# The opening of a two-stack kernel: shift and scale made in pairs, three unread products between pairs

## The reference

```
mod_lat = (silu_c @ ada_w[i] + ada_b[i])[:, None, :]      # 1024 x 6144, for c; the same for c_ctx
sh1, sc1, g1, sh2, sc2, g2 = jnp.split(mod_lat, 6, axis=-1)
h_lat = modulate(rmsnorm(x, norm_g[i, 0]), sh1, sc1)      # x * (1 + scale) + shift
h_ctx = modulate(rmsnorm(xc, norm_g[i, 0]), csh1, csc1)
y_ctx, y_lat = hybrid_na_sgu(h_ctx, h_lat, hyb_w_in[j], na_rpb[j], sgu_w[j], ...)
```

## Time and profile before

| | us |
|---|---|
| median of three runs | 2248.11 |
| the profiled execution | 2253.68 |
| its span | 2251.9 |
| TensorE busy | 2053.9 (91%) |
| VectorE busy | 1228.3 (55%) |
| ScalarE busy | 965.0 (43%) |
| GpSimd busy | 458.7 (20%) |
| mean granted clock of TensorE | 0.947 of full |

### The profile page before, as it was taken

The page is one execution under the profiler, slowest core; times in us unless marked ns, Lnnn a source line. Parts: engine busy times, 40 slices in busy tenths (PEclk is TensorE's granted clock), DMA queues, the critical chain, the costliest instruction groups (busy, mean ns, idle before and its releaser), DMA issues.

```text
span 2251.9 us, 34578 instructions
## 1 busy us (share of the span) xinstructions
PE 2053.9 (91%) x13471; PEld 1792.0 (80%) x13471; DVE 1228.3 (55%) x1706; ACT 965.0 (43%) x1527; POOL 458.7 (20%) x430
## 2 busy tenths in 40 slices
PE   2999979999999699999899979998799999789997
PEld 1677647777778489999799969988799989478997
DVE  1445455542454645667576857556644457875443
ACT  1534425322332432176474544366443343655343
POOL 2200013420342000021031510000082500006180
PEclk9899989999999899999999989999899999579999
DMA  9341223456432133222344444422255534023452
GB/s 300 116 164 57 101 105 131 169 170 212 151 126 89 56 115 110 76 94 94 113 161 166 169 148 169 161 102 89 99 178 177 169 131 152 18 74 133 169 170 92
DMA packets 44431, 297.00 MB, mean 132 GB/s; under 512 B 5200, under 2 KB 6480, under 8 KB 12048
## 3 DMA queue, kind: packets, MB, share of 16 engines
q1 hardware_dynamic: 36144, 245.38, 31.7%
q10 hardware_dynamic: 6336, 44.65, 5.7%
q0 software_dynamic: 1824, 5.16, 0.7%
HBM read 294.13 MB, written 1.05 MB: 131 GB/s over the span
## 4 chain that ended last, share of the span: by engine, by line
PE 82%; DVE 8%; ACT 4%; DMA 3%; POOL 2%; issue 2%; SPq 0%; ACTq 0%; POOLq 0%; DVEq 0%
PE acc L437 22%; PE acc L439 21%; PE acc L438 21%; PE wk L548 2%; DMA w_raw<-in_w_hyb_g 2%; PE acc L432 2%; PE acc L433 2%; PE acc L434 2%; PE wk L673 1%; PE wk L569 1%; PE wk L1407 1%; DVE w_lo L374 1%; DVE rstd L709 1%; ACT w_hi L365 1%; PE wk L1137 1%
## 5 line engine op out<-in xcount | busy, mean ns | idle before, releaser
L437 PE MATMUL acc<-Hhi,w_hi 128*128 128x272 f32 (+2 forms) x2320 | 749.7, 323 | 55.2 <-DVE Hlo L716 38.1
L374 DVE TENSOR_TENSOR w_lo<-w_raw,w_hi 128x1024 fp32r<-128x1024 f32 (+1 forms) x468 | 601.3, 1325 | 307.4 <-ACT w_hi L365 307.2
L439 PE MATMUL acc<-Hhi,w_lo 128*128 128x272 f32 (+2 forms) x2320 | 731.4, 315 | 0.0
L438 PE MATMUL acc<-Hlo,w_hi 128*128 128x272 f32 (+2 forms) x2320 | 730.4, 315 | 0.0
L365 ACT ACTIVATE w_hi<-w_raw 128x1024 fp32r<-128x1024 f32 (+1 forms) x468 | 451.2, 1013 | 384.9 <-PE acc L439 303.7
L437 PEld LDWEIGHTS acc<-Hhi,w_hi 128*128 128x128 f32 x2320 | 447.2, 193 | 96.8 <-issue 58.1
L438 PEld LDWEIGHTS acc<-Hlo,w_hi 128*128 128x128 f32 x2320 | 447.6, 193 | 21.4 <-issue 0.5
L439 PEld LDWEIGHTS acc<-Hhi,w_lo 128*128 128x128 f32 x2320 | 446.6, 192 | 22.3
L437 PE MATMUL acc<-Fhi,w_hi 128*128 128x272 f32 (+2 forms) x864 | 270.0, 312 | 6.9 <-POOL Flo L877 4.3
L439 PE MATMUL acc<-Fhi,w_lo 128*128 128x272 f32 (+2 forms) x864 | 268.1, 310 | 0.0
L438 PE MATMUL acc<-Flo,w_hi 128*128 128x272 f32 (+2 forms) x864 | 267.2, 309 | 0.0
(11 more groups left out here) (326 smaller groups left out, 2656.6 us busy)
## 6 DMA issues: line engine op xcount, KB each, us to landing
w_raw<-in_w_ffn_in SPq DMA_DIRECT2D x44, 1024.0 KB, 4.8
ada_ring<-in_w_ada ACTq DMA_DIRECT2D x40, 1024.0 KB, 4.8
w_raw<-in_w_mlp_in SPq DMA_DIRECT2D x32, 1024.0 KB, 4.8
w_raw<-in_w_mlp_out SPq DMA_DIRECT2D x32, 1024.0 KB, 4.8
w_raw<-in_w_ffn_out SPq DMA_DIRECT2D x32, 704.0 KB, 4.1
ada_first<-in_w_ada SPq DMA_DIRECT2D x8, 1024.0 KB, 31.0
w_raw<-in_w_ret_v SPq DMA_DIRECT2D x8, 1024.0 KB, 4.7
w_raw<-in_w_ret_g SPq DMA_DIRECT2D x8, 1024.0 KB, 4.8
```

Source lines behind the costliest of these rows:

```text
L374: dve.tensor_tensor(w_lo[:, r, a:b], w_raw[:, r, a:b], w_hi[:, r, a:b].bitcast(F32), ALU.subtract).then_inc(lo_done, 1)
L437: pe.matmul(o, w_hi[:, r, w], x_hi(k), start=k == 0, stop=False)
L438: pe.matmul(o, w_hi[:, r, w], x_lo(k), start=False, stop=False)
L439: mm = pe.matmul(o, w_lo[:, r, w], x_hi(k), start=False, stop=k == last)
```

## The change

1. X is issued first on SyncE's queue instead of second on ScalarE's. The eight ada slots follow in another order: slot s of the order is table slot s // 2 for even s, and 4 more for odd s. So each pair of loads holds the shift and the scale of the same two chunks. hyb_g's first slot stands ahead of the last pair, its second behind it. The ada slots lie at other addresses and no longer over H.
2. TensorE takes a pair at a time: products of both slots, columns of both. After each of the first three pairs it does three matmuls of `cvec` (32 columns) with a chunk of X (512 columns) into a bank whose content nobody reads (`WARM`).
3. VectorE adds the bias and makes the gains for the two chunks of a pair, and ScalarE and VectorE make these two chunks of H before they turn to the next pair (`act_first_norm`, `dve_first_norm`). `split_first` comes after the third pair.
4. The bias rows and late constants wait until six ada slots are used, the constants now first, and `rpb_up` lies elsewhere. The six flips are inside hyb_g's second slot, one after each of the units 9 to 14. ScalarE copies them ahead of its last GELU of hyb_g.
5. The ring's first two loads are issued after the first norm instead of after the flips. Counts of waits on `s_gain` and `s_mod` are higher by three.

```diff
@@ -220,7 +220,8 @@
-        ada_first = [at("ada_first0", [P, 4, SLOT], A), at("ada_first1", [P, 4, SLOT], h0)]
+        ada_first = [at(f"ada_first{i}", [P, SLOT], o) for i, o in enumerate(
+            (nt0 + 18 * KB, A + 50 * KB, A, A + 8 * KB, A + 16 * KB, A + 24 * KB, A + 34 * KB, A + 42 * KB))]
@@ -350,6 +351,8 @@
                     g = p.slot0 + s
+                    if g == 0:
+                        continue
@@ -455,12 +458,12 @@
             act.dma_start(vec[:], t["vec"]).then_inc(s_vec, 16)
-            act.dma_start(X[:, :, :], t["x"]).then_inc(s_x, 16)
...
+            pool.wait_ge(ada_used, 6)
@@ -488,20 +492,28 @@
-        ADA_FIRST, ADA_SLOTS = 8, 24
+        ADA_FIRST, ADA_SLOTS, WARM = 8, 24, 3
         ADA_HYB, ADA_OUT, ADA_RING = 6, 12, 40
-        ADA_READ = {0: 1, ADA_HYB: 2, ADA_OUT: 3}
+        ADA_READ = {0: 4, ADA_HYB: 5, ADA_OUT: 6}
...
-        def load_ada_first(sp):
+        def ada_slot(s):
+            return s // 2 + 4 * (s % 2) if s < ADA_FIRST else s
+        def load_opening(sp):
+            sp.dma_start(X[:, :, :], t["x"]).then_inc(s_x, 16)
             for s in range(ADA_FIRST):
-                sp.dma_start(ada_first[s // 4][:, s % 4, :], t["w_ada"][s]).then_inc(ada_loaded[s // 2], 16)
+                if s == ADA_FIRST - 2:
+                    sp.dma_start(w_raw[:, 0, 0:layers[0].width], t["w_" + layers[0].name][0]).then_inc(w_loaded[0], 16)
+                sp.dma_start(ada_first[s][:, :], t["w_ada"][ada_slot(s)]).then_inc(ada_loaded[s // 2], 16)
...
         def load_ada_ring(act):
-            act.wait_ge(s_flip, 6)
+            act.wait_ge(ada_used, ADA_FIRST)
@@ -528,7 +540,7 @@
             if s < ADA_FIRST:
-                w = ada_first[s // 4][:, s % 4, :]
+                w = ada_first[s][:, :]
@@ -564,18 +576,23 @@
                 pe.wait_ge(s_mod, ADA_READ[s - ADA_FIRST])
+            if s < ADA_FIRST and s % 2 == 0 and s > 0:
+                pe.wait_ge(s_mod, s // 2)
             for c in range(2):
-                m = 2 * s + c
+                m = 2 * ada_slot(s) + c
...
         def pe_ada_first(pe):
-            for s in range(ADA_FIRST + 1):
-                if s < ADA_FIRST:
+            for i in range(ADA_FIRST // 2):
+                for s in (2 * i, 2 * i + 1):
                     pe_ada_products(pe, s)
-                if s >= 1:
-                    pe_ada_columns(pe, s - 1)
+                for s in (2 * i, 2 * i + 1):
+                    pe_ada_columns(pe, s)
+                if i < 3:
+                    for _ in range(WARM):
+                        pe.matmul(wk[0:32, 0, :], cvec[:, 0, :], X[:, 0, :], start=True, stop=True)
@@ -613,9 +630,19 @@
-        def dve_mod_first(dve, link):
-            dve.wait_ge(ada_done, ADA_FIRST)
-            dve_mod(dve, link, 0, 0, 16, [0])
+        def dve_mod_first(dve, i):
+            def pair(x):
+                return x.rearrange("p (a m) s -> p a m s", a=2)[:, :, 2 * i:2 * i + 2, :]
+            bias = V("ada_b", 0, 16).rearrange("p (m s) -> p m s", s=1).to_broadcast([P, 16, 2])
+            dve.wait_ge(ada_done, 2 * i + 2)
+            dve.tensor_tensor(pair(mod[:, 0, 0:16, :]), pair(wk[:, 3, 0:32].rearrange("p (m s) -> p m s", s=2)), pair(bias),
+                              ALU.add).then_inc(s_mod, 1)
+            dve.wait_ge(s_mod, i + 1)
+            for s in range(2):
+                ins = dve.scalar_tensor_tensor(gains[:, 0, 0, s, 2 * i:2 * i + 2], mod[:, 0, 8 + 2 * i:10 + 2 * i, s], 1.0,
+                                               V("norm_g", 2 * i, 2), ALU.add, ALU.mult)
+            ins.then_inc(s_gain, 1)
@@ -723,6 +750,56 @@
                 lo(DC - 1)
+        def act_first_norm(act):
+            n = T1
...
+            for i in range(4):
+                act_ada(act, 2 * i, 2 * i + 2)
+                act.wait_ge(s_gain, i + 1)
+                for c in (2 * i, 2 * i + 1):
+                    act.wait_ge(nt_ready, c + 1)
+                    if c >= 2:
+                        act.wait_ge(h_ready, c - 1)
+                    for s, a, b in BOTH:
+                        ins = act.activation(n32[:, c % 2, a:b], nt[:, c % 2, a:b], ACT.Identity, scale=ada_gain(0, 0)(s, c),
+                                             bias=ada_shift(0, 0)(s, c))
+                    ins.then_inc(n32_ready, 1)
+                    act.wait_ge(n32_ready, c + 1)
+                    act.activation(H_hi[n][:, c, 0:n], n32[:, c % 2, 0:n], ACT.Copy).then_inc(hhi_ready, 1)
+                if i == 2:
+                    split_first(act)
+        def dve_first_norm(dve):
+            n = T1
+            dve.wait_ge(root_ready, 1)
+            dve.reciprocal(rstd[:, 0:n], root[:, 0:n]).then_inc(rstd_ready, 1)
+            dve.wait_ge(rstd_ready, 1)
+            def scaled(c):
+                if c >= 2:
+                    dve.wait_ge(n32_ready, c - 1)
+                dve.tensor_tensor(nt[:, c % 2, 0:n], X[:, c, 0:n], rstd[:, 0:n], ALU.mult).then_inc(nt_ready, 1)
+            scaled(0)
+            scaled(1)
+            for i in range(4):
+                dve_mod_first(dve, i)
+                for c in (2 * i, 2 * i + 1):
+                    dve.wait_ge(hhi_ready, c + 1)
+                    dve.tensor_tensor(H_lo[n][:, c, 0:n], n32[:, c % 2, 0:n], H_hi[n][:, c, 0:n].bitcast(F32),
+                                      ALU.subtract).then_inc(h_ready, 1)
+                    if c + 2 < DC:
+                        scaled(c + 2)
+                if i == 2:
+                    split_first(dve)
@@ -1095,7 +1172,6 @@
             pe.wait_ge(s_bias, N_BIAS)
-            pe.wait_ge(root_ready, 1)
@@ -2268,9 +2344,9 @@
             act_c(act)
-            act_norm(act, 0, meanwhile=lambda: (split_first(act), act_ada(act, 0, ADA_FIRST)))
-            act_rpb(act, 0, 3)
-            act_gelu(act, "hyb_g", g_sb, after=lambda s: (act_rpb(act, 3, 6), load_ada_ring(act)) if s == 0 else None)
+            act_first_norm(act)
+            load_ada_ring(act)
+            act_gelu(act, "hyb_g", g_sb, during=lambda s, c: act_rpb(act, 0, 6) if (s, c) == (1, 1) else None)
@@ -2314,7 +2390,7 @@
             dve_c(dve)
-            dve_norm(dve, 0, meanwhile=lambda: (split_first(dve), dve_mod_first(dve, link)))
+            dve_first_norm(dve)
@@ -2365,8 +2441,8 @@
             link = chain(pool, "pool")
+            load_late_constants(pool)
             load_biases(pool)
-            load_late_constants(pool)
@@ -2384,9 +2460,9 @@
             pe_ada_first(pe)
-            pe_rpb(pe, 0, 3)
             hyb = (lambda k: H_hi[T1][:, k, :], lambda k: H_lo[T1][:, k, :])
-            project(pe, "hyb_g", *hyb, need=h_need(pe, 0), after=lambda s: pe_rpb(pe, 3, 6) if s == 0 else None)
+            project(pe, "hyb_g", *hyb, need=h_need(pe, 0),
+                    fill=lambda s, j: pe_rpb(pe, j - 9, j - 8) if s == 1 and 9 <= j < 15 else None)
```

More of the change, by code:

```diff
@@ L242, in stack_kernel @@
         rpb = at("rpb", [P, 8, 6, GRID_W], A + 40 * KB)
-        rpb_up = at("rpb_up", [P, 8, 6, GRID_W], A + 78 * KB)
+        rpb_up = at("rpb_up", [P, 8, 6, GRID_W], A)
         sgu_w = at("sgu_w", [P, 8, P], A + 52 * KB)
@@ L607, in dve_mod @@
                               ALU.add).then_inc(s_mod, 1)
-            dve.wait_ge(s_mod, {(0, 0): 1, (0, 16): 2, (0, 28): 3, (0, 40): 4, (1, 0): 5}[layer, m0])
+            dve.wait_ge(s_mod, {(0, 16): 5, (0, 28): 6, (0, 40): 7, (1, 0): 8}[layer, m0])
             for s in range(2):
@@ L689, in act_norm @@
             if j < 3:
-                act.wait_ge(s_gain, (1, 3, 5)[j])
+                act.wait_ge(s_gain, (4, 6, 8)[j])
             for c in range(DC):
@@ L725, in dve_norm @@
                 lo(DC - 1)
+        def act_first_norm(act):
+            n = T1
+            act.wait_ge(s_vec, 16)
+            act.wait_ge(s_x, 16)
+            for c in range(DC):
+                if c >= 2:
+                    act.wait_ge(nsq_used, c - 1)
+                act.activation(sq[:, c % 2, 0:n], X[:, c, 0:n], ACT.Square).then_inc(nsq_ready, 1)
+            act.wait_ge(nsq_used, DC)
+            act.activation(root[:, 0:n], wk[:, 0, 0:n], ACT.Sqrt, bias=V("eps"), scale=1.0 / D).then_inc(root_ready, 1)
+            for i in range(4):
[19 more added lines that the diff above has]
+            def scaled(c):
+                if c >= 2:
+                    dve.wait_ge(n32_ready, c - 1)
[12 more added lines that the diff above has]
+                    split_first(dve)
         def h_need(pe, j):
@@ L794, in dve_residual @@
             n, x0, groups, (layer, j), _ = RES[r]
-            dve.wait_ge(s_gain, (2, 4, 5, 5)[r])
+            dve.wait_ge(s_gain, (5, 7, 8, 8)[r])
             dve.wait_ge(yroot_ready, r + 1)
@@ L1129, in pe_attn_scores @@
                 pe.wait_ge(sgu_gated, 4)
-                pe.wait_ge(s_mod, 2)
+                pe.wait_ge(s_mod, 5)
             if tt == 0:
@@ L2262, in _ @@
         def _(sp):
-            load_ada_first(sp)
+            load_opening(sp)
             stream_weights(sp)
```

## The result

| | us |
|---|---|
| median before, runs of the same chip | 2252.79 (2247.86 to 2254.25, five runs) |
| median after | 2236.02 (2235.07 to 2240.31, five runs) |
| ratio | 0.9937, 95% interval 0.9922 to 0.9952 |
| the profiled execution after, and its span | 2236.02, 2234.3 |
| mean granted clock | 0.951 (0.947 before) |

The change is faster by 14 to 17 us. That is more than this kernel's 0.3%, and a little over half of the 28 us forecast. 2236.02 lies one microsecond above the range. The kernel before is at 2252.79 over its five runs, 4.7 above the 2248.11 from which the forecast subtracted: with this base the same gain would have given 2225, so the gain is the figure to judge by.

The account below looks back on a forecast made before the run. The opening was bound by waiting until 51.8 us for hyb_g's first slot, then half-clock work. The landmark moves from 104.6 to 76.4, gaining 28 us: span 2251.9 to 2224, carried to the median as 2220 (range 2211 to 2235).

Parts of the forecast that it names:

- `flip`: Last constant on the scalar queue: lands at about 15.0 us, 15.5 with start-up; bounds 9 and 21.4.
- chunk 0: First chunk of H: ScalarE starts it at 31.2 us, after norm, reciprocal and first modulation.
- pairs: Ada slots taken two at a time, ScalarE setting the pace: 5.15 us per pair.
- hyb_g: TensorE enters this weight's work at 48.0 us, after the pairs, the split and pair 3's copies and columns.
- 411 GB/s for long rows plus a price for short ones: Opening loads: vec and X land at 8.2 us at 411 GB/s; short-row `flip` takes 6.8 more for taking turns.
- The queue is then almost alone, so I take 5 and count nothing: GpSimd's bias rows, issues ending at 56.5 us: land 5 us later, before TensorE needs them at 65.8; no cost.
- crowded end: Last bias row landing 22.5 us after issue, as crowded rows had: 79.0 us, 13 us lost.
- C: GpSimd's issues held up while VectorE makes H, landing at 77: TensorE waits 11, gain 17, 2231 us; chance 0.13.
- F: Slower: same place as C at full price, GpSimd's 26 issues taking 1.9 us each eat the gain; chance 0.03.
- the landmark: First transpose of the gating, after hyb_g and two units of hyb_qk0: at 76.4 us, against 104.6 before.
- the forecast's units and flips: hyb_g's second slot: 10.9 us plus six flips at 0.86, ending at 75.0; two more units reach 76.4.
- Rival B: Clock falls between the pairs: one fall at pair 1 delays hyb_g about 8 us; gain 18, 2230; chance 0.22.

Follow-up runs that it names:

- e5: The kernel before, with only X moved to be first on SyncE's queue; 2253.76 us, ratio 1.0010 to the kernel before.
- e3: The changed kernel, with ScalarE issuing the two ring loads only after the six flips; 2228.37 us, ratio 0.9905 to the kernel before.
- e2: e1, with the bias rows waiting for four used ada slots instead of six; 2223.19 us, ratio 0.9877 to the kernel before.
- e7: e2, with the split of hyb_g's first slot moved to after the first pair's copies; 2221.85 us, ratio 0.9869 to the kernel before.
- e8: e7, with the nine unread products spread over the gaps; 2222.84 us, ratio 0.9879 to the kernel before.
- e1: The changed kernel, with GpSimd issuing the bias rows ahead of the late constants; 2225.34 us, ratio 0.9892 to the kernel before.
- e4: e2 without the nine unread products; 2224.68 us, ratio 0.9889 to the kernel before.
- e9: e7 without the nine unread products; 2223.88 us, ratio 0.9885 to the kernel before.

## Why the prediction was wrong

**Right: the opening up to hyb_g.** `flip` at 15.54 (15.5), chunk 0 at 31.85 (31.2), pairs 5.28 and 5.55 apart (5.15), hyb_g at 49.48 (48.0). 411 GB/s for long rows plus a price for short ones was a good way to count, but that 15.5 was met to the tenth is luck: X landed at 9.9 (8.2 forecast), and `flip` 5.6 us behind it (6.8 and 0.5 forecast). X's own move did nothing for the end (e5). It was the 1.5 MB of bias rows that had held up everything.

**Wrong: the landing of the bias rows.** The failed step is "The queue is then almost alone, so I take 5 and count nothing". It took 21.9 us. The forecast had both numbers in hand, 4.8 quiet and 22.5 crowded. Its crowded end, 79.0, is 0.4 from the 78.6 at which the last row landed, yet no chance was given to it: C and F reach such a time only by late issues. And the forecast had itself moved hyb_qk0's load from 55 to 47 and the ring's from 92 to about 52, into the 11 us in which the bias rows are issued. It checked whether each of these loads was in time, and not what they would do to the rows beside them. For `flip` it had charged this kind of price, in its paragraph on X and the constants. The cost is 9.9 us of waiting and, as the clock is at half from 72.8 to 83.0 and TensorE comes back in it, 2.3 more: from the first flip to the landmark it is 12.9 us, where the forecast's units and flips came to 10.6.

**The rest.** hyb_g started 1.5 us late (0.65 of it at chunk 0, the rest in the pairs), and 1.5 more come from half clock at 48.9 to 52.3, behind an idle gap of 1.70 us. 1.5 + 1.5 + 9.9 + 2.3 = 15.2, and 91.6 - 76.4 = 15.2.

**Rival C had the size and not the cause.** It gave a wait of 11 us and 2231, against 9.9 and 2236. But it wanted GpSimd's issues held up by VectorE. They took 0.66 us each while VectorE was busy 4.61 of 5 us. e3, e2 and e7 show the cause: the same issues land in at most 21.9 us with two other queues at work, 12.1 with one fewer, 6.0 with almost none, and 13.2 when hyb_qk0's load is moved back among them (e7). That the engines alternate packet by packet isn't seen in any row; only that company costs this much. The Trainium skill, page "DMA: Bandwidth & Descriptors", section "Queues, rings and completion order", says that each engine goes round its queues a packet at a time. These landings agree with it, and by it a packet of 256 B rows waits at each turn for packets of 8 KB rows.

**Rival B.** Among six profiled kernels with unread products the clock held through the ada work in four (after, e2, e7, e8) and fell in two (e1, e3), and it came back by itself. The fall in e1 cost 3.3 us at hyb_g's start, a third of the price of 10. Without the products it fell in both (e4, e9), and the landmark came 2.2 and 4.6 us later. In e4 and e9 the first fall began in an idle gap of 4.80 us, which the products cut to 2.24 or 2.25; of the five kernels with such a gap two fell even so (e1, e3), and e8, which has 0.53 there, didn't. That is what the change has them do, but two kernels against six don't prove it, and how much they give in time isn't settled: 1.5 and 2.0 us between medians, less than the runs of one kernel differ by.

**From landmark to end.** The profiled gain at the end is 17.6 us (span) against 12.9 at the landmark. No edit is known to explain the 4.7. What follows the landmark is the same work in all twelve profiled kernels but for the times of a few loads, and it took between 2141.1 us (e5) and 2147.4 (the kernel before). The offset between the two executions grows in steps: 13.5 us at the first load of ffn_out, 15.2 at ab_qk's and 17.3 at mlp_out's. Between the first two of these the clock of the kernel before was at half from 1295.4 to 1298.9, where the other's held. So one profile of each can be some 6 us off here, and the changed kernel's span is only 10.3 us above the 2224 of the forecast, with a landmark 15.2 late, because this part happened to run faster.

**Open.** The pairs with the bias rows at the very start weren't tried, as their places in memory overlap the ada slots. Neither the length of the bias rows nor the engine that issues them was varied, so how much of the 21.9 us comes from short rows, and how much from 5 MB of company and fifteen of their own kind ahead of the last, isn't separated. Which of e2, e7 and e8 is best can't be told; e7's median beats both the kernel before (by 30.0 us, ratio 0.9869) and the changed one.

## What to carry to other kernels

When a load is moved, count what it does to the loads it now meets, not only whether it is in time itself; a load of 96 KB in short rows lost up to 17 us here, as much as the 1 MB loads beside it, so issue short rows into a stretch where the DMA engines are idle. Before a rearrangement of an opening, try the one line that delays transfers that nobody needs yet: here it gave at least as much as the whole change. A duration taken from a row holds only for the company in which it was measured.

## What the runs showed of the hardware

- 1.5 MB in rows of 256 B keep the DMA engines busy 0.94 to 0.99 at 118 to 148 GB/s (e2, 35 to 45 us), where long rows move 411 to 423. A load of this kind takes as much of the engines as about three times its bytes in long rows.
- The clock can stay at half under light ada work: 0.50 with TensorE busy 4.34 of 5 us in e9, and 12.00 of 12.00 in the earlier trace rows. In e1, with unread products among it, it came back within 7 us (35.8 to 42.5); but in e4, without them, it came back between two falls as well. What decides this isn't settled.
- GpSimd's issues weren't slowed by VectorE's f32 products and subtractions: 662 ns at the median, with 692 the longest, beside a VectorE busy 4.61 of 5 us (45 to 50 us of the changed kernel).
- Of five kernels in which TensorE stood idle for 2.24 or 2.25 us before the second pair's columns, two lost the full clock there, e1 inside the gap and e3 1.4 us behind it; in the changed kernel, e2 and e7 it held.
